# Differential attention: the squares of heads 0 to 5 split into a rounded part and a remainder, and summed by rounded matmuls

## What is computed

```python
def diff_attend(q, k, v, lam):
    ...
        s = jnp.einsum('bqhmd,bkhmd->bhmqk', qi, k).astype(jnp.float32) * scale
        p = jax.nn.softmax(s, axis=-1)
        a = (p[:, :, 0] - lam * p[:, :, 1]).astype(v.dtype)
        return jnp.einsum('bhqk,bkhd->bqhd', a, v)

def da_output(o, subln_w, lam_init, w_o):
    of = o.astype(jnp.float32)
    of = of * lax.rsqrt(jnp.mean(jnp.square(of), axis=-1, keepdims=True) + EPS) * subln_w
```

## Time and profile before

| | us |
|---|---|
| median of 3 runs | 1761.77 |
| lowest, highest | 1761.27, 1763.57 |
| the profiled execution | 1758.15 |
| its span in the trace | 1756.4 |

### The profile page before, as it was taken

The page is one execution under the profiler, slowest core; times in us unless marked ns, Lnnn a source line. Parts: engine busy times, 40 slices in busy tenths (PEclk is TensorE's granted clock), DMA queues, the critical chain, the costliest instruction groups (busy, mean ns, idle before and its releaser), DMA issues.

```text
span 1756.4 us, 30164 instructions
## 1 busy us (share of the span) xinstructions
PE 1694.3 (96%) x11440; PEld 1592.0 (91%) x11440; DVE 1080.1 (61%) x1760; ACT 703.7 (40%) x1142; POOL 638.7 (36%) x317
## 2 busy tenths in 40 slices
PE   6999999899999999999999999999999999999996
PEld 4888888598989999889998899998899999999996
DVE  2676777757855416667368654646878761477824
ACT  4455555537322212223246554644463321233324
POOL 4222111356442333233554222124745333233344
PEclk8999999999999999999999999999999999999998
DMA  9312222521544213543211112111202222222221
GB/s 360 131 59 72 67 62 84 202 84 54 188 177 163 83 66 111 200 183 121 74 65 55 64 55 82 64 55 40 94 25 84 72 78 78 72 72 72 85 83 60
DMA packets 59768, 170.96 MB, mean 97 GB/s; under 512 B 7944, under 2 KB 20488, under 8 KB 59664
## 3 DMA queue, kind: packets, MB, share of 16 engines
q1 hardware_dynamic: 51584, 163.33, 26.6%
q10 hardware_dynamic: 8080, 6.18, 1.1%
HBM read 161.07 MB, written 4.74 MB: 94 GB/s over the span
## 4 chain that ended last, share of the span: by engine, by line
PE 68%; DVE 10%; ACT 7%; issue 4%; DVEq 4%; POOL 4%; ACTq 1%; DMA 1%; SPq 0%; POOLq 0%
PE pj L761 57%; POOL wlo L633 3%; ACT pr L1578 2%; PE psO L1013 2%; PE mO L1246 2%; PE pfrow L786 1%; DVEq L2308 1%; PE psS L978 1%; DVE pr L2322 1%; POOL ss L647 1%; DVE sm L2307 1%; ACTq L1439 1%; ACT whi L1384 1%; ACT h32t L1438 1%; PE mS L1202 1%
## 5 line engine op out<-in xcount | busy, mean ns | idle before, releaser
L591 POOL TENSOR_TENSOR wlo<-wraw,whi 128x1024 fp32r<-128x1024 f32 (+1 forms) x120 | 311.1, 2592 | 772.1 <-ACT whi L1384 769.9
L761 PE MATMUL pj<-Hh,whi 128*128 128x320 f32 x2240 | 533.7, 317 | 11.0 <-ACT Hh L1559 4.0
L761 PE MATMUL pj<-Hh,wlo 128*128 128x320 f32 x2240 | 517.0, 310 | 0.0
L761 PE MATMUL pj<-Hl,whi 128*128 128x320 f32 x2240 | 515.3, 310 | 0.9 <-POOL Hl L620 0.7
L761 PEld LDWEIGHTS pj<-Hh,whi 128*128 128x128 f32 x2240 | 373.9, 189 | 36.4 <-issue 26.4
L761 PEld LDWEIGHTS pj<-Hl,whi 128*128 128x128 f32 x2240 | 376.8, 188 | 1.4 <-POOL Hl L620 1.0
L761 PEld LDWEIGHTS pj<-Hh,wlo 128*128 128x128 f32 x2240 | 377.2, 189 | 0.3
L1384 ACT CAST whi<-wraw 128x1024 fp32r<-128x1024 f32 (+1 forms) x168 | 187.1, 1113 | 263.9 <-PE pj L761 227.7
L2228 DVE SCALAR_TENSOR_TENSOR fcv<-fus,vec,fcv 128x127 f32<-128x127 f32 (+1 forms) x176 | 222.4, 1304 | 15.1 <-issue 15.1
L2090 DVE SCALAR_TENSOR_TENSOR X<-pj,mods,X 128x128 f32<-128x128 f32 (+5 forms) x114 | 43.1, 433 | 205.8 <-PE pj L761 205.5
L761 PE MATMUL pj<-Gh,whi 128*128 128x320 f32 x704 | 168.3, 310 | 0.8 <-POOL wlo L633 0.8
(11 more groups left out here) (367 smaller groups left out, 2358.3 us busy)
## 6 DMA issues: line engine op xcount, KB each, us to landing
wraw<-in_w_up SPq DMA_DIRECT2D x84, 512.0 KB, 3.5
fwr<-in_w_ada SPq DMA_DIRECT2D x56, 512.0 KB, 6.0
wraw<-in_w_dn SPq DMA_DIRECT2D x32, 704.0 KB, 4.1
wraw<-in_w_qkv SPq DMA_DIRECT2D x24, 512.0 KB, 3.4
wraw<-in_w_mlin SPq DMA_DIRECT2D x24, 512.0 KB, 3.4
awr<-in_w_ada SPq DMA_DIRECT2D x16, 512.0 KB, 10.4
awr<-in_w_ada SPq DMA_DIRECT2D x16, 256.0 KB, 7.9
wraw<-in_w_wo SPq DMA_DIRECT2D x8, 512.0 KB, 3.5
```

What stands on the lines that cost most here:

```text
L591: nc.gpsimd.tensor_tensor(wlo[k][:, 0:width], wraw[k][:, 0:width], whi[k][:, 0:width].bitcast(F32), ALU.subtract).then_inc(w_lo, 1)
L761: last = mm(out[:, c, 0:HALF], w, x[:, j, c * HALF:(c + 1) * HALF], start=(j == 0 and n == 0), stop=(j == n_k - 1 and n == 2))
```

## The change

In heads 0 to 5 (`SPLIT_SQUARES = DA_HEADS - 2`) ScalarE writes the squares three times: as before in fp32 to `ss`, and in two halves of 320 columns rounded to fp32r (`sqh`). GpSimd subtracts the rounded halves from `ss` and writes the remainder, fp32r, to `sql`; it does so behind the weight split of unit 3h + 4, the key's. TensorE sums `sqh` and `sql` by rounded matmuls with a rounded matrix of ones, `onesr`, which VectorE makes once. `sqh` and `sql` lie in the unused columns of the weight buffers, so that no memory is added beyond `onesr`. `osq_ready` is now given by GpSimd in these heads, and a new semaphore `osq_hi` counts ScalarE's halves. The loop of weight splits on GpSimd is written out. Heads 6 and 7 stay as they were.

```diff
+SPLIT_SQUARES = DA_HEADS - 2
...
+            sqh = [whi[k][:, D:D + HALF] for k in range(2)]
+            sql = [wlo[k][:, D:D + HALF] for k in range(2)]
+            onesr = sb("onesr", [P, P], F32R, s)
...
-            split_run(U_QKV + 2, 3 * DA_HEADS, D)
+            def square_lo(h):
+
+                for c in range(2):
+                    pool.wait_ge(osq_hi, 2 * h + c + 1)
+                    last = nc.gpsimd.tensor_tensor(sql[c], ss[:, cols_of(c)], sqh[c].bitcast(F32), ALU.subtract)
+                last.then_inc(osq_ready, 1)
+
+            split_one(U_QKV + 2, D)
+            split_one(U_QKV + 3, D)
+            for h in range(DA_HEADS):
+                split_one(3 * h + 4, D)
+                if 0 < h <= SPLIT_SQUARES:
+                    square_lo(h - 1)
+                if h + 1 < DA_HEADS:
+                    split_one(3 * h + 5, D)
+                    split_one(3 * h + 6, D)
...
                 for c in range(2):
-                    last = mm(psT[:, c, 0:HALF], ones[:, :], ss[:, c * HALF:(c + 1) * HALF], start=True, stop=True)
+                    if h < SPLIT_SQUARES:
+                        mm(psT[:, c, 0:HALF], onesr[:, :], sqh[c], start=True, stop=False)
+                        last = mm(psT[:, c, 0:HALF], onesr[:, :], sql[c], start=False, stop=True)
+                    else:
+                        last = mm(psT[:, c, 0:HALF], ones[:, :], ss[:, c * HALF:(c + 1) * HALF], start=True, stop=True)
...
             def o_square(h):
                 act.drain()
-                fn(ss[:, :], O32[:, h, :], ACT.Square).then_inc(osq_ready, 1)
+                if h < SPLIT_SQUARES:
+                    fn(ss[:, :], O32[:, h, :], ACT.Square)
+                    for c in range(2):
+                        fn(sqh[c], O32[:, h, cols_of(c)], ACT.Square).then_inc(osq_hi, 1)
+                else:
+                    fn(ss[:, :], O32[:, h, :], ACT.Square).then_inc(osq_ready, 1)
...
             q_lo(0)
+            dve.wait_ge(ones_ready, 1)
+            ts(onesr[:, :], ones[:, :], 1.0, None, ALU.mult)
             k_lo(0)
```

More of the change, by code:

```diff
@@ L391, in hybrid_step @@
         ckc_hi = sem("ckc_hi")
-        o_full, o_free, osq_ready, onorm, rms_ready = (
-            sem(n) for n in ("o_full", "o_free", "osq_ready", "onorm", "rms_ready"))
+        o_full, o_free, osq_ready, osq_hi, onorm, rms_ready = (
+            sem(n) for n in ("o_full", "o_free", "osq_ready", "osq_hi", "onorm", "rms_ready"))
         (wg_in, wg_clear, tri_in, wgh_ready, wg_ready, g_done, g_copied, gate_steps, ln_ready, gx_ready,
```

## The result

The change makes the kernel slower by 0.2%: 1765.09 us median against 1761.29 before, +3.8 us; the ratio is 1.0020, with a 95% interval of 1.0012 to 1.0028 (+2.1 to +4.9 us). The forecast was 1766.8 us, +5.0. The ratios come from a comparison of the single runs; they can differ from the quotient of two medians by up to 0.0005.

A forecast was written before the change was run, and what follows sets the result against it. TensorE, nearly full, and VectorE's chain were taken to bound the kernel in turns. +5.4 us at turn(h, 1), -0.4 at turn(h-1, 4) and 0 for the rest gave +5.0 on 1761.77, so 1766.8 us, range 1762.5 to 1770.5.

The forecast's parts named there:

- likeliest case: GpSimd's subtractions collide with VectorE's rotation of q: 1766.8 us, own range 1766.1 to 1768.5; chance 0.66.
- case 3: Only one subtraction costs, because the squares come at another moment: +2.0 us, 1763.8; chance 0.13.
- case 1: Main case, the subtractions collide with VectorE's rotation of q: +4.3 to +6.7 us; chance 0.66.
- point A: Transposes of turn(h, 1), waiting for VectorE's combination without slack: 0.9 us later in each of six heads, +5.4 us.
- point B: Transposes of turn(h-1, 4), behind rms(h-1): of 0.56 us saved only 0.07 a head comes through, -0.4 us in six.
- handed-over durations: Operations of VectorE or GpSimd that waited for the port end 0.13 to 0.15 us sooner than free ones; delay 0.78, not 1.19.
- 115 ns: Skill's time from release to the blocked side's start; over three handovers 0.35 us a head, 2 us in all; not adopted.
- ScalarE's squares: Two extra squares add 0.7 us a head under ScalarE's 1.24 us wait before the copy of k: nothing.
- The rest: onesr's 0.2 us hides under 1.04 us of VectorE idle time, and GpSimd's written-out loop costs nothing: 0.
- (2): GpSimd keeps the port for both subtractions before VectorE gets it: +7.2 to +8.9 us, some 1769.5; chance 0.10.
- (4): Nothing happens: the collision is absorbed and the matmul saving stays hidden, 1761.8 us; chance 0.06.
- (5): The matmul saving comes through and the collision doesn't occur: -3.4 us, 1758.4; chance 0.05.

The follow-up runs named there:

- e1: The change without GpSimd's two subtractions, TensorE summing the rounded squares twice; 1759.96 us, 0.9988 of the kernel before.
- e3: The change with its squares and subtractions, but TensorE summing the fp32 squares by plain matmuls; 1766.20 us, 1.0020 of the kernel before.
- e9: The change with only the first of the two subtractions, the rounded second half summed twice; 1762.31 us, 1.0004 of the kernel before.
- e5: The change with squares made earlier and both subtractions laid beneath VectorE's nmax reductions, which read PSUM; 1760.26 us, 1.0001 of the kernel before.
- e2: The kernel before plus ScalarE's two extra squares, the written-out loop and an unused onesr; 1760.06 us, 0.9989 of the kernel before.
- e10: The kernel before with GpSimd's loop of weight splits written out and nothing else; 1761.86 us, 0.9999 of the kernel before.
- e4: The kernel before, loop written out, with GpSimd's split of unit 3h+6 held until combine(h, 4) is done; 1760.92 us, 0.9994 of the kernel before.
- e7: The change, subtractions left in place, with the split of unit 3h+6 held until combine(h, 4) is done; 1761.33 us, 1.0000 of the kernel before.
- e6: The change with subtractions moved beneath VectorE's reductions and the split of unit 3h+6 held until combine(h, 4); 1756.75 us, 0.9978 of the kernel before.
- e11: The changed kernel unaltered, run once more; 1765.49 us, 1.0024 of the kernel before.

## Why the prediction was right, and by how much its terms were off

**The number.** The measured 1765.09 us lies inside the stated range, 1762.5 to 1770.5, but below the likeliest case's own range (1766.1 to 1768.5) and it is nearer to case 3 (1763.8) than to the forecast (1766.8). By the bounds that the prediction set for its chances, 1758.2 to 1765.3 as no change, it even falls just inside "same", to which it gave 0.25, though the interval of the ratio excludes no change. The number alone would not bear out case 1; the periods and the rows do. The forecast owes part of its nearness to two errors of opposite sign: point A was put 0.8 us too high in the six heads and point B's saving some 0.2 to 0.3 too high.

**What bounds.** The two meeting points were right. e1 and e3 separate them: in their traces, without the subtractions point A has no wait, and with plain matmuls point B has none.

**Point A.** The mechanism is shown by e1 (gone without the subtractions), e9 (half of it with one of them, in the unequal parts that the turns give) and e5 (gone with both, laid elsewhere). Its size was given as 0.78 with handed-over durations and 1.19 with free ones; 0.77 is what the timeline shows, and 0.76 the period. I took 0.9, toward the other end, although I had written myself that these operations are handed over. That is the mis-sized term: six times 0.76 are 4.6 us, not 5.4. The steps inside held too: the rotation's sum (L2348 before, L2377 in the changed kernel) was to end 0.51 late and took 1.20 instead of 0.69; the one-operand reciprocal passed beneath a subtraction (220.51 in the timeline above, while L696 ran to 221.15).

The 115 ns after each release, which would have added 2 us as an estimate by the Trainium skill ("SBUF — State Buffer", section "A bandwidth-pool intuition that's wrong (but worth ruling out)"), where they were measured with a DMA, are not there: in e9 VectorE's held operation ends 0.55 us after GpSimd's, less than its 0.69 alone. The measurement decides, and it is the handed-over value.

**Point B.** 0.4 us were to come through, 0.07 a head; the runs show 0.03 a head between e3 and the change and 0.02 between e2 and e1. TensorE's part was right, with 0.66 instead of 0.59 for the new rms. Another 0.02 to 0.03 of the 0.07 go on VectorE's side: the weight split beneath which VectorE is held at point B takes 2.39 or 2.40 us in heads 1 to 5 of e1, e5 and the change, and 2.36 to 2.38 in before, e10, e2 and e3, whose matmuls are plain. The prediction took its length as fixed. Why it is longer is not known.

**ScalarE's squares.** 0.7 us under a wait of 1.24: what is left of the wait is 0.51 in the change and 0.53 in e2, whose period is that of before. The cover was real.

**The rest.** onesr, the written-out loop (e10) and the new wait on osq_hi cost nothing that shows.

**The sum.** Six times 0.76, the change's period less that of before, are +4.6 us, with point B's part in it; the medians give +3.8 (2.1 to 4.9), at equal clock +3.6 to +3.9. Most of the difference has a place. From head 6's q rotation to the last rms are 65.55 us in before and 65.56 in e10, and 64.92 in e1 and 64.89 in e5; the granted clock is 1.00 throughout in these four. (In the traces of the change and of e2 it falls on the way, so they can't be laid beside them.) That is 0.6 to 0.7 us less in kernels with the two extra squares, and it lies in two waits, before turn_v(7) and before rms(6), the latter 1.05 us in before and e10, 0.74 in e1 and e5 and 0.79 in the change. In the last head, TensorE waits 1.03 us for VectorE before turn_v(7) in the kernel before, in e4 and in e10, and 0.74 or 0.75 in the change and in every experiment that has ScalarE's two extra squares. The rows ahead of it are ScalarE's copy of v, its DMA issue and the next cast, in before and in e2:

```profile
314.66 0.69 ACT L1390 COPY v<-pj 128x640 f32<-128x640 f32 x1 [0.46 <-PE pj L761]
315.70 0.34 ACTq L1611 DMA_DIRECT2D out_cache_vT<-v  x1
316.08 0.69 ACT L1589 CAST Ah<-psT 128x640 fp32r<-128x640 f32 x1 [0.73 <-PE psT L994]
```

```profile
313.12 0.69 ACT L1408 COPY v<-pj 128x640 f32<-128x640 f32 x1 [0.46 <-PE pj L779]
313.87 0.34 ACTq L1629 DMA_DIRECT2D out_cache_vT<-v  x1
314.25 0.69 ACT L1607 CAST Ah<-psT 128x640 fp32r<-128x640 f32 x1 [0.45 <-PE psT L1012]
```

The issue starts 0.35 us after the copy's end in the one and 0.06 after it in the other, with the same instructions around it. It explains the first of the two waits. So some 0.6 of the 0.8 and 1.0 us by which e1 and e2 lie under before are in the traces, and the rest is within the uncertainty; e5 lies only 0.1 under its before, which is within it too. If the change has the same 0.6 less, which its two waits suggest, the sum is +4.0. Why that issue is late in the programs with fewer ScalarE instructions, and what shortens the second wait, stays open; no run here was made for it.

**The rivals.** That GpSimd keeps the port for both subtractions (2) is excluded by the rows above: VectorE's L2377 ended at 220.42 and the second subtraction at 221.15. (Its upper end was mis-added: with free durations the rotation's sum would end 1.65 us late, not 1.55, so +9.5 and not +8.9; nothing hangs on it.) That only one costs (3), that nothing happens (4) and that the saving comes through (5) fall with the periods. e7 and e6 show what (5) would have needed: not a faster matmul alone, but the combination 2.1 us sooner.

## What to carry to other kernels

Work that fits into an engine's idle time is not free if it takes a port that a full chain uses: lay GpSimd's elementwise work beneath reductions of VectorE that read PSUM, as e5 does (other operations on PSUM were not tried), or hold it by a wait until one of them runs. Before an operation of TensorE is made faster, look at what the next meeting point waits for and what holds that up; here one wait on a semaphore, put in front of a weight split that wasn't urgent, turned a saving that was hidden into one that counts (from 0.02 or 0.03 to 0.32 us a head). Compare kernels that differ by a few tenths of a per cent by the period of a repeating stage in the trace first, and by medians only after allowing for the granted clock.

## What the runs showed of the hardware that was not expected

The run-to-run scatter of this kernel is mostly the granted clock: between 0.987 and 0.994 in its runs, at 1.05 us for each 0.001, so that a median of ten runs can stand 1 to 2 us away from another's for that reason alone (e9's by 2.4). Part of it is a fall to the lower level behind a wait of 1.36 us that comes in some executions and not in others (e11). A VectorE scale of two elements, L2316, was held until the end of a split in e4: it took 1.08 us from 93.95 where it takes 0.17 alone (206.87 to 207.04 in the change, L2338). What an operation loses at the port depends on what is running, not on its own size. It has only one operand of data, so the prediction's words, "reads two operands in SBUF", do not name everything that is held. The port alternated between the two engines in all six heads of the change alike: the rotation's sum took 1.20 us and the one-element product 0.41 in each.
